# Expert weights of a two-layer mixture by halves: each 0.5 MB half of a chunk is loaded and given back by itself, and the buffers of the first round are dealt out differently

## The reference, cut to what matters

```python
y = jnp.zeros_like(t)
for g in range(N_GROUPS):
    a = jnp.einsum('nd,edf->nef', t, w_gate[g])
    b = jnp.einsum('nd,edf->nef', t, w_up[g])
    hid = jax.nn.silu(a) * b * combine[:, g, :, None]
    y = y + jnp.einsum('nef,efd->nd', hid, w_down[g])
```

## Time and profile before

| | |
|---|---|
| median of 3 runs | 1374.11 us (1372.82 to 1382.52) |
| profiled execution: its time, its span | 1378.85 us, 1377.0 us |
| mean granted TensorE clock | 0.980 |
| TensorE, VectorE, ScalarE busy | 1282.9, 658.2, 548.3 us |
| SyncE's DMA queue | 69440 packets, 335.51 MB |
| expert loads of 1 MB (L407), of 0.5 MB (L411) | 164, 56 |
| their median time from issue to landing | 18.1, 17.9 us |

### The profile page before, as it was taken

One profiled execution on the slowest core, in us unless ns is written; L12 is line 12 of the kernel. 1 busy time (PEld: TensorE's weight loads), 2 busy tenths in 40 slices (PEclk: granted clock), 3 DMA queues, 4 the chain that ended last, 5 costly groups with the idle time before them and its releaser, 6 DMA issues.

```text
span 1377.0 us, 19011 instructions
## 1 busy us (share of the span) xinstructions
PE 1282.9 (93%) x7252; PEld 929.0 (67%) x7252; DVE 658.2 (48%) x1283; ACT 548.3 (40%) x1072; POOL 49.7 (4%) x84
## 2 busy tenths in 40 slices
PE   7999899999997899999998799999889988999986
PEld 5878899998876799999777544444367864443432
DVE  6656666666857566666756511111056563110102
ACT  5355544446455554444666221111055641111101
POOL 0000000000003000000300000000020000000000
PEclk9999999999999999999999899999999898999999
DMA  9532455554650365555423969999974195999995
GB/s 348 184 123 91 152 187 184 183 183 134 203 182 1 126 207 181 183 186 185 164 87 151 368 266 421 421 420 420 422 265 147 63 386 217 423 421 422 420 421 234
DMA packets 69610, 336.80 MB, mean 245 GB/s; under 512 B 8928, under 2 KB 9056, under 8 KB 48416
## 3 DMA queue, kind: packets, MB, share of 16 engines
q1 hardware_dynamic: 69440, 335.51, 64.8%
q0 software_dynamic: 96, 0.30, 0.1%
HBM read 334.72 MB, written 1.05 MB: 244 GB/s over the span
## 4 chain that ended last, share of the span: by engine, by line
PE 78%; DVE 7%; DMA 7%; ACT 4%; issue 2%; SPq 1%; POOL 0%; DVEq 0%; POOLq 0%; ACTq 0%
PE bank L1439 16%; PE bank L1441 15%; PE bank L1440 15%; PE bank L1759 13%; PE bank L1786 6%; DMA expert_part<-stream 5%; PE bank L1716 2%; DVE w_low L869 2%; DMA raw<-stream 1%; PE bank L1602 1%; PE bank L1799 1%; PE bank L1498 1%; PE bank L1541 1%; DVE x_low L888 1%; PE bank L1800 1%
## 5 line engine op out<-in xcount | busy, mean ns | idle before, releaser
L869 DVE TENSOR_TENSOR w_low<-raw,w_high 128x1024 fp32r<-128x1024 f32 (+1 forms) x246 | 285.3, 1212 | 122.8 <-ACT w_high L524 122.6
L524 ACT ACTIVATE w_high<-raw 128x1024 fp32r<-128x1024 f32 (+1 forms) x246 | 241.3, 1042 | 32.3 <-PE bank L1441 30.9
L1759 PE MATMUL bank<-expert_part,slots_x 128*64 128x512 f32 x1024 | 233.3, 593 | 9.4 <-DMA expert_part<-stream 8.1
L1439 PE MATMUL bank<-x_high,w_high 128*128 128x256 f32 (+1 forms) x712 | 202.6, 285 | 4.0 <-DVE x_low L888 3.8
L1440 PE MATMUL bank<-x_low,w_high 128*128 128x256 f32 (+1 forms) x712 | 202.1, 284 | 0.0
L1441 PE MATMUL bank<-x_high,w_low 128*128 128x256 f32 (+1 forms) x712 | 202.0, 284 | 0.0
L1759 PEld LDWEIGHTS bank<-expert_part,slots_x 128*64 128x64 f32 x1024 | 76.9, 137 | 159.3 <-issue 138.0
L1439 PE MATMUL bank<-w_high,x_high 128*128 128x512 f32 (+1 forms) x416 | 163.9, 394 | 8.3 <-DVE x_low L888 3.5
L1441 PE MATMUL bank<-w_high,x_low 128*128 128x512 f32 (+1 forms) x416 | 161.4, 388 | 0.0
L1440 PE MATMUL bank<-w_low,x_high 128*128 128x512 f32 (+1 forms) x416 | 161.3, 388 | 0.0
L1189 DVE SCALAR_TENSOR_TENSOR expert_hid<-expert_gate,combine,bank 128x256 f32<-128x256 f32 x32 | 15.4, 481 | 305.2 <-ACT expert_gate L682 305.2
(11 more groups left out here) (274 smaller groups left out, 1576.5 us busy)
## 6 DMA issues: line engine op xcount, KB each, us to landing
expert_part<-stream SPq DMA_DIRECT2D x164, 1024.0 KB, 18.1
raw<-stream SPq DMA_DIRECT2D x244, 512.0 KB, 5.2
expert_part<-stream SPq DMA_DIRECT2D x56, 512.0 KB, 17.9
const_sb<-const SPq DMA_DIRECT2D x1, 2070.0 KB, 13.5
residual<-x SPq DMA_DIRECT2D x2, 512.0 KB, 4.0
final_gain<-fgain SPq DMA_DIRECT2D x2, 512.0 KB, 8.7
out<-residual SPq DMA_DIRECT2D x2, 512.0 KB, 2.6
small_sb<-small SPq DMA_DIRECT2D x1, 765.0 KB, 5.9
```

The lines of the kernel that those rows point to most:

```text
L524: nc.scalar.activation(wh[:, u, cols], raw[:, u, cols], ACT.Copy).then_inc(w_high, 1)
L869: tt(wl[:, u, cols], raw[:, u, cols], wh[:, u, cols].bitcast(F32), ALU.subtract).then_inc(w_low, 1)
L1439: mm(o, ah, bh, start=start, stop=False, **kw)
L1759: ins = mm(B[0][half * CAP:(half + 1) * CAP, :], xg[p // 4 % 2][:, k, x_of], w[k % 4 // 2][:, k % 2 * 512:(k % 2 + 1) * 512], start=k == 0 ...
```

## The change

The parts of the first round are dealt to the places so that parts 0 and 1 lie in places 9 and 10, which are used again, and place 15, which is not, holds part 9. The places are still loaded in the same order; other parts lie in them. Every part is loaded by two transfers of 0.5 MB, each with its own wait in front of it. `part_used` now counts halves: it goes up after every odd k of `up` and after each of the two k of `down`'s second column half, 12 times a pair, and `used(l, i, half)` gives the count at which a half is free. TensorE waits for each half of every part. VectorE computes the overflow flag and gives `route_ready` right after `route`, ahead of the first `slots_odd`.

```diff
-FIRST_ROUND = [ONCE_RESULT, 9, 10, ONCE_SLOTS_X, 11, 14, 0, 1, 2, 3, 4, 5, 6, 7, 8, 12, 13]
-HOISTED = [1, 2, 4]
-FIRST_LOADS = [0, 5, 6, 7, 8, 9, 10, 11, 12, 13, 14, 3, 15, 16]
+FIRST_ROUND = [9, 10, 11, ONCE_SLOTS_X, 14, 0, 1, 2, 3, ONCE_RESULT, 4, 5, 6, 7, 8, 12, 13]
+HOISTED = [0, 1, 2]
+FIRST_LOADS = [9, 4, 5, 6, 7, 8, 10, 11, 12, 13, 14, 3, 15, 16]
...
+def used(l, i, half):
+    return 2 * (LAYER_PARTS * l + i - i % 2) + 2 * half + i % 2 + 1
...
                 if earlier_in_slot(i):
-                    sync.wait_ge(part_used, LAYER_PARTS * l + earlier_in_slot(i)[-1] + 1)
+                    pass
...
-                if in_one[at]:
-                    sync.dma_start(whole[at][:, :], stream[c]).then_inc(slot_in[at][0], 16)
-                    return
                 for half in range(2):
                     lo = half * CH // 2
+                    if earlier_in_slot(i):
+                        sync.wait_ge(part_used, used(l, earlier_in_slot(i)[-1], half))
                     sync.dma_start(slot[at][half], stream[c][:, lo:lo + CH // 2]).then_inc(slot_in[at][half], 16)
...
                 route(l)
-                for j in (1, 3):
-                    slots_odd(0, j, B[4 + j])
-                combined(0)
-                picks(1)
 
                 f = route_f
...
                 nc.vector.tensor_copy(route_i[:, 0:1], rw[:, 0, 0:1]).then_inc(route_ready, 1)
+
+                for j in (1, 3):
+                    slots_odd(0, j, B[4 + j])
+                combined(0)
+                picks(1)
...
                 def arrived(i, half):
-                    if half == 0 or not in_one[slot_of(i)]:
-                        pe.wait_ge(slot_in[slot_of(i)][half], 16 * loads_of(l, i))
+                    pe.wait_ge(slot_in[slot_of(i)][half], 16 * loads_of(l, i))
...
-                            if k % 4 == 3:
+                            if k % 2:
                                 ins.then_inc(part_used, 1)
...
-                            if k and col:
+                            if col:
                                 ins.then_inc(part_used, 1)
```

More of the change, by code:

```diff
@@ L375, in load @@
                 if S_LAYER[1] <= c < S_LAYER[1] + RING:
-                    sync.wait_ge(part_used, last_part(u) + 1)
+                    sync.wait_ge(part_used, used(0, last_part(u), 1))
                 for part in range(2):
@@ L484, in _ @@
                 if l:
-                    pool.wait_ge(part_used, last_part(14) + 1)
+                    pool.wait_ge(part_used, used(0, last_part(14), 1))
                 pool.dma_start(router_raw, router[l]).then_inc(router_in, 16)
@@ L516, in split @@
                 if S_LAYER[1] <= c < S_LAYER[1] + RING:
-                    act.wait_ge(part_used, last_part(RING + u) + 1)
+                    act.wait_ge(part_used, used(0, last_part(RING + u), 1))
                 if c >= RING or not isinstance(off, int):
@@ L678, in moe @@
                     q, g = p // 2, p // 4
-                    act.wait_ge(part_used, LAYER_PARTS * l + PARTS * p + 4)
+                    act.wait_ge(part_used, used(l, PARTS * p + 3, 1))
                     if p0 + p:
@@ L695, in moe @@
                         else:
-                            act.wait_ge(part_used, LAYER_PARTS * l + PARTS * (p + 1))
+                            act.wait_ge(part_used, used(l, PARTS * p + 5, 1))
                         nc.scalar.activation(ys_high[:, half * 512:(half + 1) * 512], B[2 + half][:, :], ACT.Copy)\
@@ L863, in split @@
                 if S_LAYER[1] <= c < S_LAYER[1] + RING:
-                    dve.wait_ge(part_used, last_part(2 * RING + u) + 1)
+                    dve.wait_ge(part_used, used(0, last_part(2 * RING + u), 1))
                 n = WIDTH.get(c, CH) // 2
@@ L2051, in _ @@
         def _(sync):
-            sync.wait_ge(part_used, LAYER_PARTS + last_part(14) + 1)
+            sync.wait_ge(part_used, used(1, last_part(14), 1))
             sync.dma_start(fg[:, :], fgain[1]).then_inc(fg_in, 16)
```

## The result

The changed kernel takes 1386.95 us (median of 5 runs, 1377.79 to 1390.89) against 1375.10 for the kernel before on the same chip (5 runs, 1372.82 to 1382.52); ratio 1.0068, interval [1.0035, 1.0101]. I had forecast 1373.5 in 1365 to 1382. It is about 12 us slower by the medians (9 by the ratio), and out of the range.

A forecast was written before the change was run, and what follows sets the result against it. Weight transfers were taken to bound the end of each layer. Rows +4.9 and refill -4.2 us in each of two layers, -2.0 once at the end, sum to -0.6: 1373.5 us on the median, range 1365 to 1382.

The forecast's parts named there:

- Transfers bound the expert stages: Expert stages of both layers: transfers at 2.487 us a part set each layer's end, so early gains and per-part costs show there.
- Rows of 4 KB, +4.9 us a layer: Expert stream: halves with 4 KB instead of 8 KB rows cost 0.068 us more a part, times 72.
- The lower bound: Expert stream: short rows might cost nothing, as 20 of 75 reloaded parts were said to come in halves already at 421 GB/s.
- rival of free halves: Expert stream: halves cost no more than wholes, -10.4 us in all, 1364 us; chance 0.12.
- Earlier refill, -4.2 us a layer: Start of each expert stage: parts 17 to 23 reloaded sooner, so part 23 lands earlier; gain 4.2 us, between 3.4 and 5.1.
- The flag earlier, more issues, more waits: nothing: VectorE's flag fits a gap, SyncE's 82 more issues a layer are covered by its waits, TensorE works ahead: no cost taken.
- rival of a starved stream: SyncE's queue: halves issued only every 1.68 us, too slow for the stream, 115 us more, 1489 us; chance 0.03.
- A fixed time for each transfer: Rival in the expert stream: 2.5 us fixed time paid twice as often; a tenth of it is +72 us, 1446 us; chance 0.02.
- The estimate by that page of the Trainium skill: Expert stream: with transfers that don't overlap, 6.4 us a part instead of 4.4, some 290 us more for both layers.
- The end of a layer, -2.0 us once: End of layer 1: only part 95's second half holds the last down products; gain 2.0 us, between 1 and 2.2; layer 0 nothing.
- The sum: Whole kernel: 2 x (4.9 - 4.2) - 2.0 = -0.6 us, 1378.2 on the profiled execution, 1373.5 on the median.
- the refill brings nothing: Rival at the expert stages: slow packets or lack of places eat the 4.2 us, +7.8 us, 1382 us; chance 0.16.

The follow-up runs named there:

- second profile: Changed kernel run again without edit, for a profile of a run near the median: 1389.83 us, ratio 1.0087; profiled execution 1389.78 us.
- second experiment: Kernel before with the new order of places and the earlier flag, transfers and giving back as before: 1379.73 us, ratio 1.0013.
- order only: Kernel before with the new order of places and the earlier flag, whole transfers and giving back by whole parts kept: 1379.73 us, ratio 1.0013.
- the two pairs with products that keep the clock up: Kernel before and changed kernel, both with useless products: seven a layer, 1388.44 and 1394.59 us; two in layer 1, 1376.97 and 1382.95 us.
- hybrid: Changed kernel, but by halves only parts 17 to 27 and 92 to 95 of a layer and places that are two halves anyway: 1380.87 us, ratio 1.0017.
- the experiments with late starts: Useless transfers ahead of layer 1's ring: kernel before with 0.5, 1, 2 MB, 1383.40, 1382.35, 1385.74 us; changed kernel with 1 MB, 1391.15 us.
- hybrid with two products: The hybrid with two useless 128x384 products among the narrow ones of layer 1's L2013: 1376.54 us, ratio 0.9992.
- before + 0.5 MB: Kernel before with one useless 0.5 MB transfer between layer 0's experts and layer 1's ring: 1383.40 us, ratio 1.0044.
- before + 1 MB: Kernel before with one useless 1 MB transfer between layer 0's experts and layer 1's ring: 1382.35 us, ratio 1.0046.
- before + 2 MB: Kernel before with two useless 1 MB transfers between layer 0's experts and layer 1's ring: 1385.74 us, ratio 1.0058.
- halves only: Kernel before with every expert part loaded by two 0.5 MB transfers, still given back as a whole, old order and flag: 1390.83 us, ratio 1.0098.
- changed again: Changed kernel run once more without edit: 1389.83 us, ratio 1.0087.
- singly, old order: Changed kernel with the old order of places and old flag position, each half still given back by itself: 1391.37 us, ratio 1.0115.
- changed + 1 MB: Changed kernel with one useless 1 MB transfer between layer 0's experts and layer 1's ring: 1391.15 us, ratio 1.0117.

## Why the prediction was wrong

**Transfers bound the expert stages.** Right for the prices, each part's showed at the end of the stage. The gains at its start did so only in part: the order alone won 2.7 and 4.0 us there and kept none and 0.4 of them at part 95.

**Rows of 4 KB, +4.9 us a layer.** Right: +5.4 and +4.6 in the changed kernel, +4.5 and +4.6 with nothing but halves. The stream with 8 KB rows in 62 of its 72 parts gives 420 to 423 GB/s, the one with rows of 4 KB 407 to 412. The lower bound, nothing, is excluded, and with it the rival of free halves. Its support was miscounted: I had read 20 transfers of 0.5 MB as 20 parts. They are ten, and the kernel before loads 11 of its 79 parts from 17 on by halves, one in seven and not a quarter; 14 of its 17 places are one piece, not 12.

**Earlier refill, -4.2 us a layer.** This step failed by its size. Part 23 came 2.9 and 2.5 us earlier, in the second profile 2.4 and 1.3. The issues were as I had them, 0.4 to 0.5 us later each (798.67 for 798.2, 800.39 for 799.9, 809.94 for 809.5). The landings were not: the first half of part 17 landed after 3.7 us, its second half after 6.2 and the second half of part 20 after 5.9 us, where I had let each take 3.8 at most. The answers of the lines view for the three issues, answering to the earlier trace rows:

```profile
L414 SPq DMA_DIRECT2D expert_part<-stream x1: 328/328/328, 798.7 to 798.7; - x1
...
DMA to landing us min/median/max: 3.7/3.7/3.7
...
L414 SPq DMA_DIRECT2D expert_part<-stream x1: 328/328/328, 800.4 to 800.4; - x1
...
DMA to landing us min/median/max: 6.2/6.2/6.2
...
L414 SPq DMA_DIRECT2D expert_part<-stream x1: 327/327/327, 809.9 to 809.9; - x1
...
DMA to landing us min/median/max: 5.9/5.9/5.9
```

For such slow packets I had allowed 1.5 us, out of the 2.3 that the old schedule lost. My schedule without them has part 23 at 821.0 - 796.6 = 24.4 us after the first product; it came after 27.4 and 27.7, so 3.0 and 3.3 us were lost, 0.4 of them by the later issues. The second half of part 17 was 2.4 us late, which the wait for part 20's place hid in part, and the second half of part 20 was 2.1 us late. The 2.3 us of the old schedule were for the most part another thing, the 1.5 us at part 22 (second experiment), and no measure for a restart. My schedule treated the refill as a list of issues with a fixed time to landing; here a queue that restarts does not give that. What makes those packets slow is open.

And what the order gains is kept only if the places keep up: with whole transfers it is lost again within ten parts (order only). That I did not foresee. In the changed kernel it cost little: its 72 parts take 183.2 to 184.8 us, against 183.6 and 183.5 with the halves alone. Against the kernel with halves alone, at part 95, order and finer giving back are worth 2.6 and 3.0 us a layer, in the second profile 1.8 and 2.1.

**The flag earlier, more issues, more waits: nothing.** Right. The pieces of up and down in the chain are 3.65 and 3.70 us as before, SyncE's longest wait for a place that the expert products give back is 4.8 us. SyncE feeds halves at 411 GB/s, so the rival of a starved stream (1489 us) is out.

**A fixed time for each transfer.** Out as well: halves land 1.28 us apart in the stream. (My sum for a tenth of it, +72 us, was twice too high even so: it charged all 288 halves, and at most half of them are additional.) The Trainium skill's rule ("DMA: Bandwidth & Descriptors", section Bandwidth: batch to 1 MiB or more) points the right way here, halves do lose; but the trace does not agree with its size. The estimate by that page of the Trainium skill was some 290 us for both layers; the halves alone cost 9.1 us over 144 parts, 2.5%. The Trainium skill gives its fixed time in Anatomy of one DMA for transfers that GpSimd issues; here SyncE issues them, into a queue that is kept filled.

**The end of a layer, -2.0 us once.** Right in kind, smaller: -1.3 us, in layer 1. I had 10 instructions, 2.3 us, left from the landing of part 95; 12 down products start behind it, and they end 2.97 us after it. In layer 0 the forecast of nothing missed the later start of layer 1, +0.4 and +0.9 us.

**The sum.** Transfers and ends were forecast at -0.6 us. In the first profile they are 5.4 + 4.6 - 2.9 - 2.5 - 1.3 + 0.4 = +3.7, in the second 5.7 + 4.3 - 2.4 - 1.3 - 1.3 + 0.9 = +5.9, and the two pairs with products that keep the clock up have +6.2 and +6.0 us. That is the rival "the refill brings nothing", +7.8, more nearly than my forecast. By itself it would have been 1380 us, inside my range; the time left the range by the clock's part.

**What I had no term for: the clock.** This is the second step that failed: I moved the sum from one profiled execution to the median by the whole difference of 4.7 us, as if the two kernels had to have the same share of runs at a low clock. About 6 of the 12 us are the same code ahead of the experts running longer at half clock, most of it layer 1's attention. The kernel before has such runs too: of its 97 executions in the four sessions, 41 have a mean clock under 0.982, and its profiled one (1378.85 us at 0.980, which I had noted and not followed up) is of this kind. In the changed kernel 10 of 11 executions are under 0.982.

That the clock is the cause of the second 6 us rests on three things. First, the length of layer 1's attention follows the time that it spends at half clock, in all 11 profiles without added products:

| at half clock in the stage, us | the stage, us |
|---|---|
| 13.7, 14.7 | 131.1, 130.5 |
| 27.3, 28.1 | 135.4, 135.8 |
| 30.7, 31.0 | 137.2, 136.2 |
| 33.5, 34.1 (three), 37.2 | 138.1, 137.2 to 138.9, 138.4 |

A straight line through them has 0.35 us for each us at half clock. Second, the difference between the kernels, 12 and 11 us by the medians and 9.4 and 12.0 by the ratios, is 6.0 and 6.2 us (5.8 and 5.9) when useless products stand there in both. Third, the hybrid gets 3 to 4 us faster by them. The second and third are small against the intervals of single ratios, and agree with each other. Why a changed start brings the long stretch more often is open; the experiments with late starts show only that other starts had other stretches.

No version beat the kernel before by more than the measurement tells: the hybrid with two products is at 0.9992 [0.9973, 1.0011].

## What to carry to other kernels

Give a stream its long rows back wherever nothing waits for the half: of this change, only some 15 of 96 parts could win by being halved, and all that had been whole paid, 82 in a layer. When a refill is scheduled on paper, count the first transfers after a pause at their slowest observed time to landing, not at that of one issued alone, and check for each step behind them whether the place is free. And where a kernel's runs fall into two groups by granted clock, find the stretch that makes the difference before predicting: a change of a few microseconds elsewhere can move the median from one group to the other.

## What the runs showed of the hardware

**The clock falls under a busy TensorE.** In the kernel before, the stretch at half clock starts 4.07 us after the narrow products of L2013 do (in the other eight profiles that have one without added products, 2.0 to 4.0 us after). This window is those 4.07 us, clock 1.00:

```profile
1083.23:1087.30 4.07, 4.07 (x36) 4.00 (x36) 0.64 (x4) 0.98 (x4) 0.00 (x0) 1.00 0.02 4
```

TensorE was busy in all of them, with 36 matmuls, all but one of 64 columns; in the other eight, too, it had no idle time in the 5 us before the fall. The Trainium skill ("TensorE: Matmul & The Clock Gate", section Why this matters for your kernels) has idle gaps as what lowers the clock mid-kernel; here there was none, and two products of 384 columns among the narrow ones took the fall away or cut it to 3.4 us.

**How long it stays low differs from profile to profile**, and the start of the narrow products alone does not tell it. Start of L2013 in layer 1, and the stretch at half clock that followed, in the profiles without added products:

| kernel | start | half clock for |
|---|---|---|
| before | 1083.23 | 10.2 |
| before + 0.5 MB | 1086.25 | none |
| hybrid | 1086.37 | 20.5 |
| order only | 1086.51 | 13.7 |
| before + 1 MB | 1086.62 | 10.2 |
| changed | 1086.68 | none |
| before + 2 MB | 1087.30 | 20.5 |
| halves only | 1088.56 | 20.5 |
| changed again | 1089.42 | 20.5 |
| singly, old order | 1089.42 | 20.5 |
| changed + 1 MB | 1089.87 | 17.1 |

Of the four that start at 1087 and later without the added megabyte in the changed kernel, all have 20.5 us; between 1086.2 and 1086.7 stand none, 10.2, 13.7 and 20.5 us. One profile a kernel cannot tell whether tenths of a microsecond decide here or something else.

**Transfers after a pause.** Where the new order starts with halves (16 starts in eight profiles), a 0.5 MB transfer into an idle queue lands after 3.5 to 3.9 us, and one issued 1.7 us behind it after 4.9 to 6.6 us, 2.8 to 4.6 us behind the one ahead of it, for 1.28 us of bytes. With whole transfers the kernel before showed 6.7 and 6.2 us for one issued 1.55 us behind two halves, where a lone one takes 4.8.

**Short rows cost at the packet.** A row of 4 KB takes 160 ns on its DMA engine and one of 8 KB 312, so two short ones take 2.6% longer than a long one, which is what the streams differ by.
